# Last feed-forward part of a two-block network: high and low stream in one product of 512 columns

## The chip, the cores and the metric

One core of a Trainium2 chip runs the whole program. The metric is the device time of one execution in microseconds; the times shown are of three runs.

## What is computed

The input is 256 tokens of 1024 features; 16 meta tokens are put ahead of them (272 in all). A first block of two layers (each: feed-forward, mixer, feed-forward) is followed by a second block with attention, a recurrent mixer and 32 routed experts. All is float32. The part that the change touches is the last feed-forward part of the second layer, and the residual around it:

```python
def swiglu(x, w_gate, w_up, w_down):
    return (jax.nn.silu(x @ w_gate) * (x @ w_up)) @ w_down

h = h + 0.5 * swiglu(rmsnorm(h, ffn2_norm[l]), ffn2_w_gate[l], ffn2_w_up[l], ffn2_w_down[l])
```

with 1024 features, 2816 hidden ones, and (here) only the 256 real tokens, since the meta tokens aren't used after it.

## The kernel before, in words

Features lie on the 128 partitions, tokens on the columns. Numbers of full precision are split for the matrix engine into a high part of type fp32r and a low part (the rest), and one product of float32 becomes three of fp32r: `product` (L741 to L745) does w_hi x_hi (L743), w_hi x_lo (L744) and w_lo x_hi (L745), all added up in one PSUM bank. Each needs a weight load of its own.

**A feed-forward part** is `ffn(f, n)` on every engine, f = 0 to 3; the last is f = 3, with `window(3)` = 16, so `t:T` are 256 columns (272 in the others). It has 22 hidden tiles j. For each the weights of gate and of up are one *half* each: a tile of 128 x 1024 in one of 7 ring slots (two halves a slot), split into one of four buffers `w_split`. Half 2j is gate, half 2j + 1 is up; a half is 8 chunks of 3 products (`features`, L773; the first two halves go chunk by chunk, `first_two`, L763). Pair j writes PSUM banks 2(j % 4) and 2(j % 4) + 1. Then come 22 *down* parts of 8 outputs times 3 products, which add into the 8 banks; the last two are done output by output (L821 to L827).

**The order of each queue is written out by hand**, and each engine works its queue in order:

- TensorE waits for the low split of a half, from pair 4 on for the eviction of the pair four before (L794), and ahead of half 4 does the norm's sum (`norm_sum`, L735), for which ScalarE squares and GpSimd adds (L2791). In pair j = 14 (`CTX_AT`) it also sums squares for the second block into bank 5, and half 29, which has that bank, waits until ScalarE has copied the sum out as `ctx_r` (L800).
- ScalarE (L1585 to L1600), per pair: at j = 14 first the copy `ctx_r` (L1590); from j = 2 on the high splits of the halves 2j + 4 and 2j + 5 (`weights_hi`, L1506, each once the half four before is used); the Silu of gate j (L1594) once VectorE has evicted it; for j = 2 to 9 the high copy of hid j - 2 (L1569).
- VectorE (L2087 to L2107), per pair: the low splits of the same two halves (`weights_lo`, L1975); the eviction of gate (L2092) and of up (L2094) from PSUM, each times 1/rms (`rstd`); a drain; once the Silu is there, hid = up x gate (L2102); for j = 2 to 9 the low copy of hid j - 2 (`hidden_lo`, L2084).
- In the down parts both go on with the splits of weights and of the other tiles of hid. At the end `residual` (L1985) adds half of each output bank to h; ScalarE squares h (L1734) for the norm of the second block, which TensorE sums with plain fp32 products (L1060), and GpSimd adds the same squares (L2856).
- GpSimd adds up squares of the context (L2843, L2846) at the start of this part.
- SyncE loads the weights, a slot at a time, once the low splits of the slot's former contents are done.

The plain fp32 products of the second block (L1066 with 512 columns, L1072 with 256, L1367 with 128) stand in the trace as two records each, and each record has a weight load.

The first lines of VectorE's eviction, as they are before:

```python
dve.wait_ge(split_used, n0 + 2 * j + 1)
nc.vector.tensor_tensor(gate_act[:, j % 4, t:T], ps[:, bank, 0:T - t], rstd[:, t:T], ALU.mult).then_inc(gate_ready, 1)
dve.wait_ge(split_used, n0 + 2 * j + 2)
used = nc.vector.tensor_tensor(hid[:, j, t:T], ps[:, bank + 1, 0:T - t], rstd[:, t:T], ALU.mult)
```

Of the kernel before, what the change touches and what calls it, by code (L numbers as in the profile page):

```python
# [14 lines left out]
C = D // P  # L15
META, SEQ = 16, 256
T = META + SEQ
DEPTH = 2
FF = 2816
F = FF // P  # L20
# [9 lines left out]
SPLITS = 4  # L30
# [8 lines left out]
HID_SPLITS = 8  # L39
# [191 lines left out]
def build(nc, stream_ffn, stream_in, stream_out, stream_mod, stream_in2, stream_out2, stream_expert,  # L231
# [4 lines left out]
    with ExitStack() as ctx:  # L236
# [3 lines left out]
        def sem(name):  # L240
            return ctx.enter_context(nc.semaphore(name))
# [47 lines left out]

        rest = 3 * C * T  # L290
        h = cut(arena, 0, C, T)
        x_hi = parts("x_hi", arena_at + 4 * C * T, C, T)
        x_lo = parts("x_lo", arena_at + 4 * 2 * C * T, C, T)
        w_split = [parts(f"w_split{b}", ring_at + 4 * (NS + b) * SLOT, 2, C, P) for b in range(SPLITS)]
        X_AT = (NS + SPLITS) * SLOT
        m = layout(ring, X_AT, [("rv", 3, 512), ("rstd", T)])
# [3 lines left out]
        m = layout(arena, rest, [("hid", F, T), ("gate", 4, T)])  # L300
        hid, gate_act = m["hid"], m["gate"]
        warm = cut(arena, rest, 513)
        hid_hi = parts("hid_hi", arena_at + 4 * (rest + (F + 4) * T), HID_SPLITS, T)
        hid_lo = parts("hid_lo", arena_at + 4 * (rest + (F + 4 + HID_SPLITS) * T), HID_SPLITS, T)
        assert rest + (F + 4 + 2 * HID_SPLITS) * T <= ARENA
        ffn_sq = hid[:, F - C:]

# [35 lines left out]
        stat_ready, dev_ready, factor_ready, normed, last_normed, back_ready, y_hi_ready, y_split_ready = (  # L343
            sem(x) for x in ("stat_ready", "dev_ready", "factor_ready", "normed", "last_normed", "back_ready", "y_hi_ready", "y_split_ready"))
        lam_dots_ready, lam_exp_ready = sem("lam_dots_ready"), sem("lam_exp_ready")


        raw2 = h[:, :, META:T]
# [376 lines left out]
        def _(pe):  # L725
# [15 lines left out]
            def product(to, w, k, hi, lo, first, last_):  # L741

                pe.matmul(to, w[:, 0, k], hi, start=first, stop=False)  # L743
                pe.matmul(to, w[:, 0, k], lo, start=False, stop=False)  # L744
                return pe.matmul(to, w[:, 1, k], hi, start=False, stop=last_)  # L745

            def split_half(n):

                pe.wait_ge(split_ready, n + 2)
                return w_split[n % SPLITS]  # L750
# [12 lines left out]
            def first_two(n, n0, banks, t=0):  # L763

                both = [split_half(n0), split_half(n0 + 1)]
                for c in range(C):
                    pe.wait_ge(x_split_ready, n * C + c + 1)
                    for k in range(2):
                        last = product(ps[:, banks[k], 0:T - t], both[k], c, x_hi[:, c, t:T], x_lo[:, c, t:T], c == 0, c == C - 1)
                        if c == C - 1:  # L770
                            last.then_inc(split_used, 1)

            def features(n, bank, t=0):  # L773

                w = split_half(n)
                for c in range(C):
                    last = product(ps[:, bank, 0:T - t], w, c, x_hi[:, c, t:T], x_lo[:, c, t:T], c == 0, c == C - 1)
                last.then_inc(split_used, 1)

            def ffn(f, n):  # L780

                n0 = HALF_AT["ffn", f, 0]
                t = window(f)
                if f == 0:
                    first_of_all(n0)
                else:
                    first_two(n, n0, (0, 1), t)
                for j in range(1, F):
                    if j == 2 and f > 0:
                        norm_sum(n)  # L790
                    if j == 3:
                        pe.wait_ge(std_ready, n + 1)
                    if j >= 4:
# [12 lines left out]
                down = n0 + 2 * F  # L806

                def part(i, o):
                    return product(ps[:, o, 0:T - t], w_split[(down + i) % SPLITS], o, hid_hi[:, i % HID_SPLITS, t:T],
                                   hid_lo[:, i % HID_SPLITS, t:T], i == 0, i == F - 1)  # L810

                for i in range(F - 2):
                    split_half(down + i)
                    pe.wait_ge(hid_split_ready, f * F + i + 1)
                    for o in (4, 5, 6, 7, 0, 1, 2, 3) if i == 0 else range(C):
                        if i == 0 and o % 2 == 0:
                            pe.wait_ge(gate_up_used, f * F + F - 3 + (o - 4) % C // 2)
# [673 lines left out]
        def _(act):  # L1491
# [42 lines left out]
            def ffn(f, n):  # L1534
# [52 lines left out]
                for j in range(F):  # L1587
                    if f == 2 * DEPTH - 1 and j == CTX_AT:
                        act.wait_ge(ctx_summed, 1)
                        nc.scalar.activation(ctx_r, ps[:, 2 * (j % 4) + 1, 0:SEQ], ACT.Copy).then_inc(ctx_std_ready, 1)  # L1590
                    if j >= 2:
                        weights_hi(n0 + 2 * j + 6)
                    act.wait_ge(gate_ready, f * F + j + 1)
                    nc.scalar.activation(gate_act[:, j % 4, t:T], gate_act[:, j % 4, t:T], ACT.Silu).then_inc(gate_act_ready, 1)  # L1594
                    if 0 <= j - 2 < HID_SPLITS:
                        hidden_hi(j - 2)
                    for half in range(2):
                        if j - half in units:
                            mod_products(units[j - half], half)
# [362 lines left out]
        def _(dve):  # L1962
# [73 lines left out]
            def ffn(f, n):  # L2036
# [50 lines left out]
                for j in range(F):  # L2087
                    if j >= 2:
                        weights_lo(n0 + 2 * j + (6 if j < F - 1 else 5))
                    bank = 2 * (j % 4)  # L2090
                    dve.wait_ge(split_used, n0 + 2 * j + 1)
                    nc.vector.tensor_tensor(gate_act[:, j % 4, t:T], ps[:, bank, 0:T - t], rstd[:, t:T], ALU.mult).then_inc(gate_ready, 1)  # L2092
                    dve.wait_ge(split_used, n0 + 2 * j + 2)
                    used = nc.vector.tensor_tensor(hid[:, j, t:T], ps[:, bank + 1, 0:T - t], rstd[:, t:T], ALU.mult)  # L2094
                    if j in PORTIONS[f]:
                        used = mod_collect(PORTIONS[f][j], bank + 1)
                    used.then_inc(gate_up_used, 1)
                    if j == F - 1:
                        weights_lo(n0 + 2 * j + 6)
                    dve.drain()  # L2100
                    dve.wait_ge(gate_act_ready, f * F + j + 1)
                    nc.vector.tensor_tensor(hid[:, j, t:T], hid[:, j, t:T], gate_act[:, j % 4, t:T], ALU.mult).then_inc(hid_ready, 1)  # L2102
                    if 0 <= j - 2 < HID_SPLITS:
                        hidden_lo(j - 2)
                    if f == 0 and j == 8:
                        lambda_weights()
                    if j - 2 in units:  # L2107
                        mod_add(units[j - 2])
# [10 lines left out]
                for o in range(C):  # L2119
                    if o < C - 1:  # L2120
                        dve.wait_ge(y_ready, f * (C - 1) + o + 1)
                    else:
                        dve.wait_ge(split_used, down + F)
                    residual(o, o, 0.5, t)
                    if o >= 1 and f < 2 * DEPTH - 1:
                        stream_lo(n + 1, o - 1)
# [869 lines left out]
```

## Time and profile before

| what | value |
|---|---|
| time, median of 3 runs | 1739.18 us (1738.33 to 1740.95) |
| span of the profiled execution | 1737.7 us, 30185 instructions |
| what lies around the span, to the median | 1.5 us |
| TensorE busy (weight loads) | 1713.1 us, 99% (1408.5 us, 81%) |
| VectorE, ScalarE, GpSimd busy | 978.2, 797.4, 169.4 us |
| mean granted TensorE clock | 0.998 |
| chain that ended last | TensorE 88%, DMA 6% |

The span runs from the first to the last instruction of one profiled execution, which has no time of its own beside it; the runs are timed apart. Engines: PE is TensorE, PEld its weight loads, DVE VectorE, ACT ScalarE, POOL GpSimd, SP SyncE. A matmul's record is longer than its pitch, since matmuls are pipelined: what counts is the distance from one start to the next. The last feed-forward part goes from about 904 us to 1094 us; its down parts start at 1032.

### The profile page before, as it was taken

Reading aid. Unit: us, or ns where it says so; the run is one execution under the profiler, and the core shown is the slowest. Engines: PE = TensorE matmul, PEld = TensorE weight load, DVE = VectorE, ACT = ScalarE, POOL = GpSimd, SP = SyncE. Lnnn points to the kernel's source line nnn. Section 1 sums busy time; section 2 is a strip of 40 time slices with the busy share of each in tenths; the row PEclk is TensorE's granted clock in tenths of the full one; section 3 lists DMA queues with packets and bytes.
Section 4 is the critical chain, followed back from the end, with each engine's and each line's share of the span. In section 5 each row is a group of like instructions: output and inputs, shape, how many; then the busy total and the mean of one; then the engine's idle time right before and its main releaser. Section 6 shows DMA issues by size and latency. Waiting matters only on the chain.

```text
span 1737.7 us, 30185 instructions
## 1 busy us (share of the span) xinstructions
PE 1713.1 (99%) x12315; PEld 1408.5 (81%) x12316; DVE 978.2 (56%) x1689; ACT 797.4 (46%) x1432; POOL 169.4 (10%) x173
## 2 busy tenths in 40 slices
PE   9999999999999999999999999999999999999998
PEld 8999998999999999998999999677764544444443
DVE  6776577678766777678778666475732111121111
ACT  6664455466656765665455445354621111111111
POOL 1000053210000100014314000100410000000000
PEclk9999999999999999999999999999999999999999
DMA  9555552244566576574336555132299999999997
GB/s 384 198 228 209 170 166 103 98 172 163 224 259 249 191 270 243 196 247 141 117 130 228 190 177 176 49 85 73 114 420 404 428 427 428 428 428 428 428 427 304
DMA packets 78817, 425.87 MB, mean 245 GB/s; under 512 B 16352, under 2 KB 32992, under 8 KB 41824
## 3 DMA queue, kind: packets, MB, share of 16 engines
q1 hardware_dynamic: 78256, 421.01, 62.3%
q10 hardware_dynamic: 432, 3.08, 0.4%
q8 instruction: 89, 1.46, 0.3%
q14 instruction: 40, 0.33, 0.1%
HBM read 423.02 MB, written 1.05 MB: 244 GB/s over the span
## 4 chain that ended last, share of the span: by engine, by line
PE 88%; DMA 6%; DVE 2%; ACT 2%; issue 1%; DVEq 0%; SPq 0%; POOL 0%; POOLq 0%; ACTq 0%
PE ps L743 18%; PE ps L745 18%; PE ps L744 18%; PE ps L1393 10%; PE ps L1444 5%; DMA ring<-stream_expert 5%; PE ps L1367 3%; PE ps L1072 2%; PE ps L1066 2%; PE ps L1078 2%; DVE w_split L1975 1%; ACT w_split L1506 1%; PE ps L1374 1%; PE ps L1375 1%; PE ps L921 0%
## 5 line engine op out<-in xcount | busy, mean ns | idle before, releaser
L1975 DVE TENSOR_TENSOR w_split<-ring,w_split 128x1024 fp32r<-128x1024 f32 x335 | 421.1, 1276 | 250.3 <-ACT w_split L1506 249.7
L743 PE MATMUL ps<-x_hi,w_split 128*128 128x272 f32 (+1 forms) x1856 | 541.7, 292 | 4.7 <-DVE arena L2171 2.1
L745 PE MATMUL ps<-x_hi,w_split 128*128 128x272 f32 (+1 forms) x1856 | 534.0, 288 | 0.0
L744 PE MATMUL ps<-x_lo,w_split 128*128 128x272 f32 (+1 forms) x1856 | 532.1, 287 | 0.0
L1506 ACT ACTIVATE w_split<-ring 128x1024 fp32r<-128x1024 f32 x335 | 345.5, 1052 | 234.7 <-PE ps L745 233.2
L743 PEld LDWEIGHTS ps<-x_hi,w_split 128*128 128x128 f32 x1856 | 350.3, 189 | 12.2 <-issue 4.8
L744 PEld LDWEIGHTS ps<-x_lo,w_split 128*128 128x128 f32 x1856 | 350.2, 189 | 0.3
L745 PEld LDWEIGHTS ps<-x_hi,w_split 128*128 128x128 f32 x1856 | 350.1, 189 | 0.0
L745 PE MATMUL ps<-hid_hi,w_split 128*128 128x272 f32 (+1 forms) x704 | 201.6, 286 | 0.0
L744 PE MATMUL ps<-hid_lo,w_split 128*128 128x272 f32 (+1 forms) x704 | 201.5, 286 | 0.0
L743 PE MATMUL ps<-hid_hi,w_split 128*128 128x272 f32 (+1 forms) x704 | 201.1, 286 | 0.0
L1393 PE MATMUL ps<-ring,arena 128*64 128x512 f32 x704 | 187.4, 594 | 3.5 <-DMA ring<-stream_expert 2.8
L1393 PEld LDWEIGHTS ps<-ring,arena 128*64 128x64 f32 x704 | 58.9, 137 | 98.7 <-issue 93.5
L2724 DVE TENSOR_TENSOR arena<-arena,ps 128x512 f32<-128x512 f32 x16 | 11.0, 687 | 217.4 <-PE ps L1393 217.4
L743 PEld LDWEIGHTS ps<-hid_hi,w_split 128*128 128x128 f32 x704 | 132.7, 189 | 0.0
L744 PEld LDWEIGHTS ps<-hid_lo,w_split 128*128 128x128 f32 x704 | 132.5, 188 | 0.0
L745 PEld LDWEIGHTS ps<-hid_hi,w_split 128*128 128x128 f32 x704 | 132.5, 188 | 0.0
L1594 ACT ACTIVATE arena<-arena 128x272 f32<-128x272 f32 (+1 forms) x88 | 37.6, 427 | 151.8 <-DVE arena L2092 151.3
L1902 ACT ACTIVATE arena<-ps,small 128x128 f32<-128x128 f32 x64 | 24.0, 456 | 163.4 <-PE ps L1367 163.4
L1582 ACT ACTIVATE ring<-ring,small 128x256 f32<-128x256 f32 x192 | 81.3, 494 | 0.0
L1444 PE MATMUL ps<-ring,arena 128*64 128x512 f32 x352 | 78.0, 595 | 0.0
L2735 DVE SCALAR_TENSOR_TENSOR ye_lo<-ps,arena,ye_hi 128x512 fp32r<-128x512 f32 x32 | 24.0, 750 | 91.4 <-ACT ye_hi L1918 76.5
(438 smaller groups left out, 2362.8 us busy)
## 6 DMA issues: line engine op xcount, KB each, us to landing
ring<-stream_ffn SPq DMA_DIRECT2D x131, 1024.0 KB, 4.9
ring<-stream_expert SPq DMA_DIRECT2D x48, 2048.0 KB, 25.1
ring<-stream_expert SPq DMA_DIRECT2D x36, 1024.0 KB, 12.6
arena<-stream_expert SPq DMA_DIRECT2D x16, 2048.0 KB, 25.5
ring<-stream_in SPq DMA_DIRECT2D x27, 1024.0 KB, 4.8
ring<-stream_mod SPq DMA_DIRECT2D x24, 1024.0 KB, 4.9
con<-stream_expert SPq DMA_DIRECT2D x8, 2048.0 KB, 26.2
ring<-stream_out SPq DMA_DIRECT2D x12, 1024.0 KB, 5.0
```

Source lines behind the costliest of these rows:

```text
L743: pe.matmul(to, w[:, 0, k], hi, start=first, stop=False)
L744: pe.matmul(to, w[:, 0, k], lo, start=False, stop=False)
L745: return pe.matmul(to, w[:, 1, k], hi, start=False, stop=last_)
L1066: last = pe.matmul(ps[:, b, 0:KEYS], w[:, c], x2n[:, :, c], start=c == 0, stop=c == C - 1)
L1072: last = pe.matmul(ps[:, b, i * SEQ:i * SEQ + SEQ], w[:, i, c], x2n[:, 0, c], start=c == 0, stop=c == C - 1)
L1367: last = pe.matmul(ps[:, 6 + half, (c % 4) * P:(c % 4) * P + P], h2t[:, t, c * P:c * P + P], sel[:, t], start=t == 0, stop=t == 1)
L1393: last = pe.matmul(ps[rows, 4 + part, 0:FE], xs[:, c, rows], w, start=c == 0, stop=c == C - 1)
L1444: last = pe.matmul(ps[rows, 6 + half, 0:512], hidT[:, f, rows], w[:, half * 512:half * 512 + 512], start=f == 0, stop=f == FE // P - 1)
L1506: nc.scalar.activation(w_split[n % SPLITS][:, 0], half_of(n), ACT.Copy).then_inc(hi_ready, 1)
L1582: last = nc.scalar.activation(to[:, c], w[:, c], ACT.Identity, scale=cc[:, c, v:v + 1])
L1594: nc.scalar.activation(gate_act[:, j % 4, t:T], gate_act[:, j % 4, t:T], ACT.Silu).then_inc(gate_act_ready, 1)
L1975: nc.vector.tensor_tensor(w[:, 1], half_of(n), w[:, 0].bitcast(fp32), ALU.subtract).then_inc(split_ready, 1)
```

## The change

In parts with `t` > 0, which is the last feed-forward part alone, high and low stream lie in one tensor, `x_both` and `hid_both`, and w_hi is multiplied with both in one product of 2 x 256 columns, which fills a PSUM bank: columns 0 to 255 for the high, 256 to 511 for the low stream. w_lo x_hi is added to columns 0 to 255. For gate and up ScalarE copies the low half of a bank to SBUF as soon as its half is done, between its splits; VectorE adds the high half to it, and multiplies by 1/rms in SBUF, in two further operations behind a drain. The low copy of hid moves ahead of the wait for the Silu. At the end VectorE adds the low half of each output bank to h, drains, and adds the high half. The mixers call `product` themselves and stay as they are.

```diff
+            def wide_product(bank, w, k, both, first, last_):
+
+                hi_last = last_ and not first
+                if not hi_last:
+                    pe.matmul(ps[:, bank, 0:2 * SEQ], w[:, 0, k], both, start=first, stop=False)
+                last = pe.matmul(ps[:, bank, 0:SEQ], w[:, 1, k], both[:, 0], start=False, stop=False)
+                if hi_last:
+                    last = pe.matmul(ps[:, bank, 0:2 * SEQ], w[:, 0, k], both, start=False, stop=True)
+                return last
...
 def features(n, bank, t=0):
                 for c in range(C):
-                    last = product(ps[:, bank, 0:T - t], w, c, x_hi[:, c, t:T], x_lo[:, c, t:T], c == 0, c == C - 1)
+                    if t:
+                        last = wide_product(bank, w, c, x_both[:, :, c, t:T], c == 0, c == C - 1)
...
 def part(i, o):
+                    if t:
+                        return wide_product(o, w_split[(down + i) % SPLITS], o, hid_both[:, :, i % HID_SPLITS, t:T], i == 0, i == F - 1)
...
 scalar, for j in range(F):
-                    if j >= 2:
-                        weights_hi(n0 + 2 * j + 6)
+                    for k in range(2):
+                        if t:
+                            act.wait_ge(split_used, n0 + 2 * j + k + 1)
+                            to = gate_act[:, j % 4, t:T] if k == 0 else hid[:, j, t:T]
+                            nc.scalar.activation(to, ps[:, 2 * (j % 4) + k, SEQ:2 * SEQ], ACT.Copy).then_inc(low_copied, 1)
+                        if j >= 2:
+                            weights_hi(n0 + 2 * j + 5 + k)
                     act.wait_ge(gate_ready, f * F + j + 1)
...
 vector, for j in range(F):
+                    if t:
+                        gate_at, up_at = gate_act[:, j % 4, t:T], hid[:, j, t:T]
+                        dve.wait_ge(low_copied, LOW_BEFORE + 2 * j + 1)
+                        nc.vector.tensor_tensor(gate_at, ps[:, bank, 0:SEQ], gate_at, ALU.add)
+                        dve.wait_ge(low_copied, LOW_BEFORE + 2 * j + 2)
+                        used = nc.vector.tensor_tensor(up_at, ps[:, bank + 1, 0:SEQ], up_at, ALU.add)
+                        dve.drain()
+                        nc.vector.tensor_tensor(gate_at, gate_at, rstd[:, t:T], ALU.mult).then_inc(gate_ready, 1)
+                        nc.vector.tensor_tensor(up_at, up_at, rstd[:, t:T], ALU.mult)
+                        if 0 <= j - 2 < HID_SPLITS:
+                            hidden_lo(j - 2)
...
 vector, the outputs
+                    if t:
+                        nc.vector.scalar_tensor_tensor(h[:, o, t:T], ps[:, o, SEQ:2 * SEQ], 0.5, h[:, o, t:T], ALU.mult, ALU.add)
+                        dve.drain()
                     residual(o, o, 0.5, t)
```

`first_two` is changed as `features` is.

## Rows read from the trace of the kernel before

**Rows 1.** Stretches: us; busy time of each engine (instructions); granted clock, DMA share, GB/s.
```profile
933.80:985.60 51.80, 51.80 (x440) 51.80 (x440) 35.82 (x55) 25.02 (x36) 0.00 (x0) 1.00 0.56 197
...
1290.00:1737.70 447.70, 435.58 (x2370) 206.90 (x2366) 73.59 (x159) 70.42 (x158) 1.42 (x2) 1.00 0.98 413
```

**Rows 2.** Timeline of TensorE, gate and up products: start us, us, instruction.
```profile
949.73 0.28 PE L743 MATMUL ps<-x_hi,w_split 128*128 128x256 f32 x1
...
951.15 0.28 PE L743 MATMUL ps<-x_hi,w_split 128*128 128x256 f32 x1
```

**Rows 3.** Chain that ended last, in order of time: start us, us, plain fp32 products.
```profile
1117.31 13.81 PE ps L1066 x32
1131.12 13.81 PE ps L1072 x64
...
1302.83 1.98 PE ps L1367 x16
1305.25 1.79 PE ps L1367 x16
```

**Rows 4.** Timeline of TensorE, the norm's sum ahead of half 4.
```profile
916.93 0.70 PE L739 MATMUL ps<-arena,con 128*128 128x272 f32 x2 [0.72 <-POOL arena L2791]
```

**Rows 5.** Timelines of ScalarE and VectorE, one pair in the steady state.
```profile
951.76 1.06 ACT L1506 ACTIVATE w_split<-ring 128x1024 fp32r<-128x1024 f32 x1 [1.32 <-PE ps L745]
954.45 0.42 ACT L1594 ACTIVATE arena<-arena 128x256 f32<-128x256 f32 x1 [1.62 <-DVE arena L2092]
954.77 0.40 ACT L1569 ACTIVATE hid_hi<-arena 128x256 fp32r<-128x256 f32 x1
955.08 1.04 ACT L1506 ACTIVATE w_split<-ring 128x1024 fp32r<-128x1024 f32 x1
...
952.85 1.22 DVE L1975 TENSOR_TENSOR w_split<-ring,w_split 128x1024 fp32r<-128x1024 f32 x1 [1.15 <-ACT w_split L1506]
954.00 0.42 DVE L2092 TENSOR_TENSOR arena<-ps,ring 128x256 f32<-128x256 f32 x1
954.33 0.41 DVE L2094 TENSOR_TENSOR arena<-ps,ring 128x256 f32<-128x256 f32 x1
954.90 0.42 DVE L2102 TENSOR_TENSOR arena<-arena 128x256 f32<-128x256 f32 x1 [0.15 <-ACT arena L1594]
```

**Rows 6.** Timeline of ScalarE, two high splits in a row.
```profile
923.38 1.99 ACT L1506 ACTIVATE w_split<-ring 128x1024 fp32r<-128x1024 f32 x2
```

**Rows 7.** Timelines of ScalarE and TensorE around half 29.
```profile
988.85 0.36 ACT L1590 ACTIVATE more<-ps 128x256 f32<-128x256 f32 x1
989.11 1.06 ACT L1506 ACTIVATE w_split<-ring 128x1024 fp32r<-128x1024 f32 x1
...
989.27 0.39 PE L743 MATMUL ps<-x_hi,w_split 128*128 128x256 f32 x1 [0.25 <-ACT more L1590]
```

**Rows 8.** Timeline of VectorE at the start of the part.
```profile
919.34 1.84 DVE L1989 RECIPROCAL ring<-ring 128x272 f32<-128x272 f32 x1
921.26 0.42 DVE L2092 TENSOR_TENSOR arena<-ps,ring 128x256 f32<-128x256 f32 x1
...
923.51 0.82 DVE L2102 TENSOR_TENSOR arena<-arena 128x256 f32<-128x256 f32 x1 [0.16 <-ACT arena L1594]
924.46 3.10 DVE L1975 TENSOR_TENSOR w_split<-ring,w_split 128x1024 fp32r<-128x1024 f32 x2
```

**Rows 9.** TensorE's timeline at the program's start, then two stretches behind it.
```profile
9.93 0.40 PE L743 MATMUL ps<-x_hi,w_split 128*128 128x272 f32 x1 [1.87 <-DVE x_lo L1980]
...
10.00:12.00 2.00, 2.00 (x9) 1.85 (x10) 1.74 (x4) 2.00 (x5) 0.00 (x0) 0.55 1.01 417
12.00:14.00 2.00, 2.00 (x11) 1.86 (x11) 1.23 (x1) 1.00 (x2) 0.00 (x0) 0.60 1.00 416
```

**Rows 10.** VectorE's timeline at the end of the part; the chain, norm's product.
```profile
1091.07 0.42 DVE L1985 SCALAR_TENSOR_TENSOR arena<-ps,arena 128x256 f32<-128x256 f32 x1 [0.28 <-PE ps L745]
...
1094.53 3.45 PE ps L1060 x16
```

More of the change, by code:

```diff
@@ L291, in build @@
         h = cut(arena, 0, C, T)
-        x_hi = parts("x_hi", arena_at + 4 * C * T, C, T)
-        x_lo = parts("x_lo", arena_at + 4 * 2 * C * T, C, T)
+        x_both = parts("x_both", arena_at + 4 * C * T, 2, C, T)
+        x_hi, x_lo = x_both[:, 0], x_both[:, 1]
         w_split = [parts(f"w_split{b}", ring_at + 4 * (NS + b) * SLOT, 2, C, P) for b in range(SPLITS)]
@@ L302, in build @@
         warm = cut(arena, rest, 513)
-        hid_hi = parts("hid_hi", arena_at + 4 * (rest + (F + 4) * T), HID_SPLITS, T)
-        hid_lo = parts("hid_lo", arena_at + 4 * (rest + (F + 4 + HID_SPLITS) * T), HID_SPLITS, T)
+        hid_both = parts("hid_both", arena_at + 4 * (rest + (F + 4) * T), 2, HID_SPLITS, T)
+        hid_hi, hid_lo = hid_both[:, 0], hid_both[:, 1]
         assert rest + (F + 4 + 2 * HID_SPLITS) * T <= ARENA
@@ L345, in build @@
         lam_dots_ready, lam_exp_ready = sem("lam_dots_ready"), sem("lam_exp_ready")
+        low_copied, LOW_BEFORE = lam_exp_ready, 1
         raw2 = h[:, :, META:T]
@@ L768, in first_two @@
                     for k in range(2):
-                        last = product(ps[:, banks[k], 0:T - t], both[k], c, x_hi[:, c, t:T], x_lo[:, c, t:T], c == 0, c == C - 1)
+                        if t:
+                            last = wide_product(banks[k], both[k], c, x_both[:, :, c, t:T], c == 0, c == C - 1)
+                        else:
+                            last = product(ps[:, banks[k], 0:T], both[k], c, x_hi[:, c], x_lo[:, c], c == 0, c == C - 1)
                         if c == C - 1:
@@ L776, in features @@
                 for c in range(C):
-                    last = product(ps[:, bank, 0:T - t], w, c, x_hi[:, c, t:T], x_lo[:, c, t:T], c == 0, c == C - 1)
+                    if t:
+                        last = wide_product(bank, w, c, x_both[:, :, c, t:T], c == 0, c == C - 1)
+                    else:
+                        last = product(ps[:, bank, 0:T], w, c, x_hi[:, c], x_lo[:, c], c == 0, c == C - 1)
                 last.then_inc(split_used, 1)
@@ L2091, in ffn @@
                     dve.wait_ge(split_used, n0 + 2 * j + 1)
-                    nc.vector.tensor_tensor(gate_act[:, j % 4, t:T], ps[:, bank, 0:T - t], rstd[:, t:T], ALU.mult).then_inc(gate_ready, 1)
-                    dve.wait_ge(split_used, n0 + 2 * j + 2)
-                    used = nc.vector.tensor_tensor(hid[:, j, t:T], ps[:, bank + 1, 0:T - t], rstd[:, t:T], ALU.mult)
+                    if t:
[9 more added lines that the diff above has]
+                            hidden_lo(j - 2)
+                    else:
+                        nc.vector.tensor_tensor(gate_act[:, j % 4], ps[:, bank, 0:T], rstd, ALU.mult).then_inc(gate_ready, 1)
+                        dve.wait_ge(split_used, n0 + 2 * j + 2)
+                        used = nc.vector.tensor_tensor(hid[:, j], ps[:, bank + 1, 0:T], rstd, ALU.mult)
                     if j in PORTIONS[f]:
@@ L2102, in ffn @@
                     nc.vector.tensor_tensor(hid[:, j, t:T], hid[:, j, t:T], gate_act[:, j % 4, t:T], ALU.mult).then_inc(hid_ready, 1)
-                    if 0 <= j - 2 < HID_SPLITS:
+                    if t == 0 and 0 <= j - 2 < HID_SPLITS:
                         hidden_lo(j - 2)
@@ L2123, in ffn @@
                         dve.wait_ge(split_used, down + F)
+                    if t:
+                        nc.vector.scalar_tensor_tensor(h[:, o, t:T], ps[:, o, SEQ:2 * SEQ], 0.5, h[:, o, t:T], ALU.mult, ALU.add)
+                        dve.drain()
                     residual(o, o, 0.5, t)
```

## The prediction

> **What bounds the kernel now.** I read the stages first, then TensorE's pitch, then who waits for whom in the last feed-forward part. In the table of stretches TensorE is busy for all 51.80 us of the gate and up products [rows 1], and from 1290 us on weight traffic runs at 413 GB/s beside TensorE; those loads are gated by work of the second block, so whatever the last feed-forward part gains or loses shifts all that follows. In the timeline twelve products of 256 columns start in 951.15 - 949.73 = 1.42 us, 118.3 ns each [rows 2]. At a granted clock of 1.00, which is 2.4 GHz [rows 1], 256 columns are 106.7 ns: 11.6 ns of each are not columns. That excess is all the change can take from TensorE, for the columns stay (3 x 256 = 512 + 256).
>
> **What it takes away.** Two products per chunk instead of three. What does one of 512 columns cost when the weights of the next are loaded beside it? No such product is in the trace. The nearest rows: the records of plain fp32 products, two cycles a column, each with a weight load. With 256 columns (213.3 ns of streaming) 13.81 us / 64 = 215.8 ns, excess 2.5; with 512 columns 13.81 / 32 = 431.6 ns; with 128 columns (106.7 ns) 1.98 / 16 = 124 or 1.79 / 16 = 112 ns, excess 5 to 17 [rows 3]. So the excess is large where streaming is about as long as the load beside it and small where it is twice as long. I take 215.8 for the 512-column product and keep 118.3 for the 256-column one: 334.1 against 354.9, **20.8 ns saved per triple**. Ends: 0 (the excess goes by columns, as 431.6 is exactly twice 215.8) and 31.2 (all at the fp32 pace: 215.8 + 107.9). A fixed excess per product would be 11.6.
>
> By the Trainium skill, TensorE: Matmul & The Clock Gate, section "Back-to-back issue gap", a warm product takes N/2.4 + 2.5 ns, so a merge would save 2.5 ns a triple; here 256 columns take 118.3, not 109.2, so the page does not describe these products.
>
> **Where that saving counts.** Not in halves 0 to 3: half 4 waits for the norm's sum, which waits for GpSimd (0.72 us idle [rows 4]), and GpSimd for squares that the change doesn't touch. Those 32 triples only lengthen the wait. A half (8 triples) then takes 2.67 us, a pair 5.35 (before 5.68).
>
> **What it adds to the other engines.** Per pair j: two ScalarE copies from PSUM, each behind a wait for its half and ahead of the weight split; on VectorE two adds in place of two evictions (same shape and place, same price), a drain, and two multiplies within SBUF. Behind ScalarE's wait stand its splits, the Silu, the hi copies and at j = 14 ctx_r; the first two lead to VectorE's next low split.
>
> The loop that decides goes from one Silu to the next, because both queues are in order. Its links before, from start to start [rows 5]: hi split to low split 952.85 - 951.76 = 1.09, low split to gate eviction 954.00 - 952.85 = 1.15, eviction to Silu 954.45 - 954.00 = 0.45, Silu to what follows it 0.32, the hi copy of hid 955.08 - 954.77 = 0.31 (only for j = 2 to 9), and hi split to hi split 1.99 - 1.05 = 0.94 [rows 6]. Sum 3.95, or 4.26 with the hi copy, against a TensorE pair of 5.68: ScalarE has over a microsecond to spare and splits run ahead.
>
> Added to the loop: two PSUM copies at 0.26 (the one such copy, ctx_r: 989.11 - 988.85 [rows 7]); the second add, 0.33 (954.33 - 954.00 [rows 5]); then until the gate multiply the add's 0.41 and a drain of 0.08 (the reciprocal ends at 919.34 + 1.84 = 921.18, the next starts at 921.26 [rows 8]). The multiply takes the eviction's 0.45 to the Silu (0.42 long [rows 5]). Together 0.52 + 0.33 + 0.49 = 1.34. **The loop becomes 5.60 us for j = 2 to 9 and 5.29 after**, against a TensorE pair of 5.35. So the spare time is gone, and a lag once made isn't made up. The low copy of hid, now ahead of VectorE's wait for the Silu, waits for ScalarE's hi copy behind that Silu; VectorE's own round grows to some 5.1 and stays below the loop. SyncE's refills wait for the low splits, but run seven slots (seven pairs, 39 us) ahead of their use, at a DMA share of 0.56 [rows 1]: cost 0.
>
> The lag is made at the start. VectorE begins pair 0 at 921.26 and reaches the splits of j = 2 at 924.46, pausing only 0.16 for each Silu [rows 8]. While GpSimd works (no longer from 933.8 on [rows 1]) a multiply within SBUF takes up to 0.82 [rows 8] instead of 0.42 [rows 5]. Pairs 0 and 1 get two more each, plus the drain: 2 x (0.15 + 2 x 0.75) = 3.3, less 0.1 of idle. Splits of j = 2 then start at 927.7, end at 930.7 (1.5 each there [rows 8]), adds and drain 0.82, multiply 0.85: Silu of j = 2 at 932.4. To the Silu of j = 13 are 8 x 5.60 + 3 x 5.29 = 60.7: **993.1**. Before it is at 988.53, one 0.32 ahead of ctx_r at 988.85 [rows 7]: 4.6 us later.
>
> That Silu matters because ScalarE copies ctx_r out of PSUM right behind it, and TensorE can't start half 29, whose bank it is, before: now 0.25 us of idle, at 989.27 [rows 7]. With the change half 29 starts 4.6 us later. I add 0.5 (between 0 and 1), since GpSimd, met by more work of VectorE, keeps it slow a little longer: **+5.1 us**. The stalls on splits in halves 8 to 28 lie within it.
>
> **Clock.** Before half 29 TensorE now stands still for nearly 5 us. At the start of the program, after 1.87 us of idle, the granted clock is 0.55 and 0.60 in the next two stretches of 2 us [rows 9]: (0.45 + 0.40) x 2 = **1.7 us** lost, at the level of 1.2 GHz. I take that; ends 0 and 2.
>
> **What is left to gain.** From half 29 TensorE sets the pace again: 15 halves and 22 down parts, 37 x 8 = 296 triples x 20.8 ns = **-6.2 us**. The banks for the first down part need pair 21's adds: at most 0.2.
>
> **The tail.** The last residuals become two operations with a drain: 0.41 + 0.08 + 0.33 = 0.82 per output against TensorE's 6 x 118 = 0.71, now 0.67 [rows 10]. Over eight outputs VectorE ends 8 x 0.82 - 7 x 0.67 = 1.9 us behind. The norm's product takes the squares one by one over 3.45 us [rows 10]; its eighth step starts 3.0 us after its first, its square is there after 1.9 + 0.45 = 2.35. Cost 0; with that cover gone 0.5.
>
> **Sum.** +5.1 + 1.7 - 6.2 = +0.6 us. It is made against the profiled span of 1737.7 us; the median, 1739.2, lies 1.5 above it and moves with it: **1739.8 us**.
>
> **Rivals.** A difference of 0.2% (3.5 us) is about what a measurement tells from none.
> - *The excess goes by columns* (or the wide product loads its weights twice, so that the change does not do what it says). Nothing is saved: +6.8, **1746.0**. For it: 431.6 = 2 x 215.8. Against: 118.3 against 215.8 / 2. Chance 0.12. It is slower from a saving under 11 ns a triple on. The page's rule is the nearest to it, 2.5 x 296 = 0.7 us saved.
> - *Fixed excess per product, and a longer loop.* 11.6 ns saved gives -3.4 instead of -6.2, in sum +3.4; and each 0.1 us that a wait or drain puts on the loop is 1.1 us at half 29, the place where it is paid: **1743.7** with 0.1. For it: the loop has no gap left, and any wait between two engines that I left out adds to it; against: the wide product has streaming enough to cover a load. Chance 0.20, four fifths of it beyond 1742.7.
> - *No lag.* If VectorE's start were not late, ScalarE's copies would go into its idle time, half 29 would be late by the added 0.8 only, and 320 + 176 = 496 triples count: -10.3 + 0.8, **1729.7**. Against: VectorE's start has next to no gaps to fill [rows 8], and the loop exceeds the pair. Chance 0.10.
> - *As forecast*, 1735.7 to 1742.7: 0.52. The remaining 0.06 is spread evenly over the three.
>
> **How the numbers follow.** Low end: 31.2 ns saved (gate and up then held by the loop of 5.29: 7 x 0.39 + 22 x 0.25 = 8.4) and no clock loss: 5.1 - 8.4 = -3.3, 1735.9. High end: the first rival, 1746. Range 1735.5 to 1746. Faster by over 0.2%: 0.10 + 0.02 = 0.12; within: 0.52 + 0.04 + 0.02 = 0.58; slower: 0.12 + 0.16 + 0.02 = 0.30.
>
> **What would show it.** A triple at 334 ns in the down part; the pair's pace 5.6 us for j below 10; Silu of j = 13 near 993; half 29 waiting some 5 us for ctx_r with a lower clock behind it; down part starting some 4 us later than 1032 and ending near 1095. Wrong if low splits run ahead of TensorE at j = 10, if the wait at half 29 stays under 2 us, or if a triple takes over 345 ns.

## The result, and where the time went

| | kernel before | changed kernel |
|---|---|---|
| median, 9 runs each | 1739.34 us | 1744.41 us |
| lowest to highest | 1738.33 to 1740.95 | 1742.70 to 1746.79 |
| span of the profiled execution | 1737.7 us | 1744.8 us (its run: 1746.55) |
| granted clock, mean of the span | 0.998 | 0.995 |

The changed kernel is slower: ratio 1.0028, with a 95% interval from 1.002 to 1.0037, or 5.1 us. The forecast was 1739.8 us, within a range that reaches to 1746.0.

The profiled execution of the changed kernel is some 2 us above its median. The norm's sum, which was at 916.93 [rows 4], is now at 919.30, 2.4 us later, and this comes from the start of the program, far ahead of the changed part. In the chains that ended last the same weight split stands at 33.41 us before and at 35.77 us after, and between 12 and 20 us TensorE is granted less clock: 0.50 in each of the two stretches of 2 us, then 0.66, where the trace of before has 0.60 [rows 9] and then 1.00. The traces of experiments 3, 6 and 7 have 1.00 in all these stretches, so this differs from one execution to the next and isn't the change's. The 2.4 us are taken off below wherever a time of after stands against one of before. In order: the split before and after, the stretch after, the norm's sum after.

```profile
33.41 1.05 ACT w_split L1506
...
35.77 1.05 ACT w_split L1525
...
16.00:20.00 4.00, 4.00 (x24) 4.00 (x24) 2.75 (x6) 4.00 (x10) 3.15 (x3) 0.66 1.02 430
...
919.30 0.70 PE L740 MATMUL ps<-arena,con 128*128 128x272 f32 x2 [0.82 <-POOL arena L2830]
```

The stretches of [rows 1], and two more around half 29 (columns as there):

```profile
933.80:985.60 51.80, 51.09 (x291) 44.27 (x290) 43.35 (x74) 28.47 (x54) 0.73 (x1) 1.00 0.53 185
985.60:995.00 9.40, 6.71 (x38) 5.59 (x37) 7.43 (x13) 5.41 (x10) 0.00 (x0) 0.99 0.54 210
995.00:1000.00 5.00, 3.30 (x10) 2.81 (x11) 2.82 (x6) 1.91 (x4) 0.00 (x0) 0.50 0.58 210
```

VectorE's busy time in the first of them has gone from 35.82 to 43.35 us. The stretch has 291 products and 290 weight loads, so a wide product doesn't load its weights twice. In the third TensorE is granted a clock of 0.50, which is its level of 1.2 GHz. The timelines of ScalarE, then of VectorE, for one pair in the steady state, answer to [rows 5]:

```profile
951.77 0.42 ACT L1618 ACTIVATE arena<-arena 128x256 f32<-128x256 f32 x1 [2.48 <-DVE arena L2123]
...
957.41 0.42 ACT L1618 ACTIVATE arena<-arena 128x256 f32<-128x256 f32 x1 [2.48 <-DVE arena L2123]
...
953.75 2.45 DVE L1999 TENSOR_TENSOR w_split<-ring,w_split 128x1024 fp32r<-128x1024 f32 x2 [0.28 <-ACT w_split L1525]
956.11 0.42 DVE L2119 TENSOR_TENSOR arena<-ps,arena 128x256 f32<-128x256 f32 x1
956.44 0.42 DVE L2121 TENSOR_TENSOR arena<-ps,arena 128x256 f32<-128x256 f32 x1
956.95 0.42 DVE L2123 TENSOR_TENSOR arena<-arena,ring 128x256 f32<-128x256 f32 x1
```

From one Silu (L1618) to the next are 957.41 - 951.77 = 5.64 us, and the Silu waits 2.48 us for the gate multiply (L2123). That multiply stands behind two low splits, two adds and a drain. The round is the loop that the prediction wrote out, and neither of its two engines is busy all the time. Then ScalarE and TensorE around half 29, where [rows 7] had 0.25 us of idle:

```profile
995.96 0.42 ACT L1618 ACTIVATE arena<-arena 128x256 f32<-128x256 f32 x1 [2.48 <-DVE arena L2123]
996.28 0.37 ACT L1609 ACTIVATE more<-ps 128x256 f32<-128x256 f32 x1
996.70 0.79 PE L752 MATMUL ps<-x_both,w_split 128*128 128x512 f32 x1 [4.40 <-ACT more L1609]
...
998.15 0.63 PE L752 MATMUL ps<-x_both,w_split 128*128 128x512 f32 x1
...
998.79 0.63 PE L752 MATMUL ps<-x_both,w_split 128*128 128x512 f32 x1
...
1001.88 0.39 PE L752 MATMUL ps<-x_both,w_split 128*128 128x512 f32 x1
```

TensorE stands still for 4.40 us until ctx_r has been copied out (L1609), and then a triple takes 998.79 - 998.15 = 0.64 us for the whole of half 29. The first product of the down parts, and what follows their last:

```profile
1040.94 0.39 PE L752 MATMUL ps<-hid_both,w_split 128*128 128x512 f32 x1
...
1102.79 1.46 PE L1079 MATMUL ps<-arena,ring 128*128 128x256 f32 x6
```

For the gate and up products at full clock a whole pair is read, since one triple is too short for the trace's steps of 0.01 us. The chain that ended last marks the end of each pair's second half:

```profile
1007.15 0.24 PE ps L753 x2
1012.73 0.24 PE ps L753 x2
...
1102.95 3.45 PE ps L1079 x16
```

1012.73 - 1007.15 = 5.58 us for 16 triples, 348.8 ns each: **6.1 ns saved** in the gate and up products. The 176 triples of the down parts take 1102.79 - 1040.94 = 61.85 us, 351.4 ns each. Before they took 1094.37 - 1031.98 = 62.39 us, so **3.1 ns** are saved there.

The account up to the norm's product, in the two profiled executions: half 29 starts 996.70 - 989.27 - 2.4 = 5.0 us later; it takes 1001.88 - 996.70 = 5.18 us instead of 2.85, 2.3 more; the 14 halves behind it give back 0.8 and the down parts 0.5. Sum +6.0; the chain has 1102.95 - 1094.53 - 2.4 = 6.0. From there to the end the kernels of this study take between 641.6 and 643.5 us, without an order that I could find. The medians are only 5.1 us apart. Part of the difference to 6.0 is the clock of half 29, which is not the same in every execution: in the trace of experiment 7 TensorE waits as long ahead of it, 4.38 us, but the half takes 998.52 - 994.07 = 4.45 us, 1.6 more than before and not 2.3:

```profile
994.07 0.50 PE L753 MATMUL ps<-x_both,w_split 128*128 128x512 f32 x1 [4.38 <-ACT more L1611]
...
998.52 0.39 PE L753 MATMUL ps<-x_both,w_split 128*128 128x512 f32 x1
```

What is left of it is within the scatter of the rest of the program.

### The profile page after: what moved, and what is told of

The parts are those of the page before. It is cut to its first block, busy times and chain, and to the rows that moved or that the text cites. A ratio compares the mean times of both kernels' runs of the same rounds, so it can differ in the third digit from the quotient of the medians.

```text
span 1744.8 us, 29277 instructions
## 1 busy us (share of the span) xinstructions
PE 1715.0 (98%) x11787; PEld 1385.6 (79%) x11788; DVE 999.9 (57%) x1741; ACT 808.6 (46%) x1476; POOL 167.7 (10%) x173
## 4 chain that ended last, share of the span: by engine, by line
PE 82%; DMA 6%; DVE 5%; ACT 3%; DVEq 2%; issue 1%; SPq 0%; POOL 0%; ACTq 0%; POOLq 0%
PE ps L744 14%; PE ps L746 14%; PE ps L745 14%; PE ps L1412 10%; PE ps L1463 5%; DMA ring<-stream_expert 5%; PE ps L752 4%; PE ps L1386 3%; DVE w_split L1999 2%; PE ps L753 2%; PE ps L1091 2%; PE ps L1085 2%; ACT w_split L1525 2%; PE ps L1097 2%; DVEq L2122 1%
## 5 line engine op out<-in xcount | busy, mean ns | idle before, releaser
L744 PE MATMUL ps<-x_both,w_split 128*128 128x272 f32 (+1 forms) x1504 | 443.1, 295 | 5.6 <-DVE arena L2210 2.1
L746 PE MATMUL ps<-x_both,w_split 128*128 128x272 f32 (+1 forms) x1504 | 435.5, 290 | 0.0
L745 PE MATMUL ps<-x_both,w_split 128*128 128x272 f32 (+1 forms) x1504 | 433.4, 288 | 0.0
L744 PEld LDWEIGHTS ps<-x_both,w_split 128*128 128x128 f32 x1504 | 284.3, 189 | 12.8 <-issue 4.8
L745 PEld LDWEIGHTS ps<-x_both,w_split 128*128 128x128 f32 x1504 | 284.6, 189 | 0.2
L746 PEld LDWEIGHTS ps<-x_both,w_split 128*128 128x128 f32 x1504 | 284.0, 189 | 0.0
L1412 PE MATMUL ps<-ring,arena 128*64 128x512 f32 x704 | 187.4, 594 | 3.4 <-DMA ring<-stream_expert 2.7
L746 PE MATMUL ps<-hid_both,w_split 128*128 128x272 f32 x528 | 152.2, 288 | 0.0
L745 PE MATMUL ps<-hid_both,w_split 128*128 128x272 f32 x528 | 152.2, 288 | 0.0
L744 PE MATMUL ps<-hid_both,w_split 128*128 128x272 f32 x528 | 151.7, 287 | 0.0
L752 PE MATMUL ps<-x_both,w_split 128*128 128x512 f32 x308 | 112.6, 402 | 5.8 <-ACT more L1609 4.4
L1618 ACT ACTIVATE arena<-arena 128x272 f32<-128x272 f32 (+1 forms) x88 | 37.6, 428 | 169.8 <-DVE arena L2128 116.0
L744 PEld LDWEIGHTS ps<-hid_both,w_split 128*128 128x128 f32 x528 | 99.4, 188 | 0.0
L745 PEld LDWEIGHTS ps<-hid_both,w_split 128*128 128x128 f32 x528 | 99.3, 188 | 0.0
L746 PEld LDWEIGHTS ps<-hid_both,w_split 128*128 128x128 f32 x528 | 99.3, 188 | 0.0
L753 PE MATMUL ps<-x_both,w_split 128*128 128x256 f32 x352 | 92.8, 284 | 0.0
```

Source lines behind the costliest of these rows:

```text
L752: pe.matmul(ps[:, bank, 0:2 * SEQ], w[:, 0, k], both, start=first, stop=False)
L753: last = pe.matmul(ps[:, bank, 0:SEQ], w[:, 1, k], both[:, 0], start=False, stop=False)
L1412: last = pe.matmul(ps[rows, 4 + part, 0:FE], xs[:, c, rows], w, start=c == 0, stop=c == C - 1)
```

## The experiments

**Theory S**: the saving is small by itself, because a product of 512 columns costs about 231 ns, nearly two of 256. **Theory L, with K**: ScalarE's lag costs TensorE its 4.4 us at one place only, the copy of ctx_r, and the clock behind it costs 2.3 us more. **Theory O**: the lag comes from the order of VectorE's work in the loop. Each had a rival. A line of after is named as it stands there; edits shift the numbers by a few.

**1. The wide products without the work they bring.**

```diff
-   nc.scalar.activation(to, ps[:, 2 * (j % 4) + k, SEQ:2 * SEQ], ACT.Copy)
...
-   nc.vector.tensor_tensor(gate_at, ps[:, bank, 0:SEQ], gate_at, ALU.add)
...
-   nc.vector.tensor_tensor(gate_at, gate_at, rstd[:, t:T], ALU.mult)
+   nc.vector.tensor_tensor(gate_act[:, j % 4, t:T], ps[:, bank, 0:T - t], rstd[:, t:T], ALU.mult)
...
-   nc.vector.scalar_tensor_tensor(h[:, o, t:T], ps[:, o, SEQ:2 * SEQ], 0.5, h[:, o, t:T], ALU.mult, ALU.add)
```

> Edit: the products of 512 columns stay, but the low halves (PSUM columns 256 to 511) are never added: ScalarE's low copies, VectorE's two adds, the drain, the multiplies in place and the extra residual step are gone, and VectorE evicts columns 0 to 255 times rstd as before the change. The output lacks the high weights times the low stream. Theory S (a triple of products saves only 5 to 6 ns, because a 512-column product costs about 231 ns by itself): the time is 496 x 5.2 ns = 2.6 us under the kernel before, 1736.5 to 1737.5, ratio to it about 0.9985; triples stand at 0.35 us in the trace and half 29 starts without the 4.4 us wait. Rival P (the 512-column product would take 213 ns, and what slows it is the extra work of ScalarE and VectorE beside it): triples at 0.334 us and 10 us under the kernel before, near 1729.

Measured: 1736.95 us against 1739.51 of before on the same chip, ratio 0.9983 (0.9974 to 0.9991). The group of TensorE's wide gate and up products from 903 to 1100 us (busy us, mean ns of one | idle before them and what ended it):

```profile
L752 PE MATMUL ps<-x_both,w_split 128*128 128x512 f32 x308 | 110.1, 395 | 0.4 <-ACT more L1609 0.3
```

Nearly nothing is waited for, and in the chain the pairs still end 5.58 us apart, with ScalarE and VectorE free of all the added work:

```profile
1002.54 0.24 PE ps L753 x2
1008.12 0.24 PE ps L753 x2
```

The wide product is not slowed by the work beside it; rival P falls. What TensorE alone can win is 2 to 3 us.

**2. All that work, with narrow products.**

```diff
-   pe.matmul(ps[:, bank, 0:2 * SEQ], w[:, 0, k], both, start=first, stop=False)
+   pe.matmul(ps[:, bank, 0:SEQ], w[:, 0, k], both[:, 0], start=first, stop=False)
+   pe.matmul(ps[:, bank, SEQ:2 * SEQ], w[:, 0, k], both[:, 1], start=False, stop=False)
```

> Edit: all of the change's work on ScalarE and VectorE stays, but the triple is three products of 256 columns again, the low one into PSUM columns 256 to 511. Theory S: half 29 is set by ScalarE, not by the products, so only the 296 triples behind it cost, 5.2 ns each: 1.5 us over the changed kernel, near 1746, and the wait before half 29 shrinks from 4.4 to about 3.2 us. Theory P or any theory in which the wide product saves 15 to 20 ns a triple that something else ate: 4.5 to 6 us over the changed kernel, near 1750.

Measured: 1746.61 us, ratio to before 1.004 (1.0027 to 1.0053): 7.1 us over before, about 2 over the changed kernel. TensorE's timeline at half 29, and the stretch around it:

```profile
996.21 0.58 PE L750 MATMUL ps<-x_both,w_split 128*128 128x256 f32 x1 [3.95 <-ACT more L1605]
...
995.00:1000.00 5.00, 3.79 (x17) 3.80 (x18) 2.41 (x4) 1.91 (x4) 0.00 (x0) 0.50 0.61 210
```

The start of half 29 and the fall of the clock are the same without a single wide product: ScalarE sets them. The wait is 3.95 us, 0.45 less than in the changed kernel, and not 1.2 less as expected. The expectation counted all 200 triples from half 4 to half 28. But in both kernels TensorE waits for a low split at 938 us, and the end of that stall is VectorE's, so only the 152 triples behind it count, 0.9 us. And in the changed kernel the pairs that follow take longer than 5.58 us. These are the last products of two of its halves, twelve halves apart:

```profile
946.49 0.39 PE L755 MATMUL ps<-x_both,w_split 128*128 128x512 f32 x1
...
980.30 0.39 PE L755 MATMUL ps<-x_both,w_split 128*128 128x512 f32 x1
```

Six pairs in 980.30 - 946.49 = 33.81 us are 5.64 us each, the round of the loop. It looks as if the low splits hold TensorE there, by less than the list of waits shows; in experiments 5 and 6, where the lag is gone, the pairs take 5.58 us. Against narrow pairs of 5.68 us seven such pairs save 0.04 us each, and the last five halves 0.05 each: 0.5 us in all, about what is measured.

**3. The copy of ctx_r one pair earlier.**

```diff
-   if f == 2 * DEPTH - 1 and j == CTX_AT:
+   if f == 2 * DEPTH - 1 and j == CTX_AT - 1:
+       pe.wait_ge(gate_up_used, f * F + CTX_AT - 3)
        pe.wait_ge(ctx_sq_ready, 1)
-       pe.matmul(ps[:, 2 * (j % 4) + 1, 0:SEQ], ones, ctx_acc, start=True, stop=True)
+       pe.matmul(ps[:, 2 * (CTX_AT % 4) + 1, 0:SEQ], ones, ctx_acc, start=True, stop=True)
```

and ScalarE's copy likewise.

> Edit: TensorE issues the ones product of the context's squares at the start of pair 13 instead of 14 (still into bank 5), and ScalarE copies it out before pair 13's work; half 29 keeps its wait for that copy. Theory L (ScalarE's lag reaches TensorE only through this copy, and costs the idle time and the clock after it): the 4.4 us wait before half 29 is gone, the granted clock stays at 0.98 or more there, and the time is 5 to 6.7 us under the changed kernel, 1738 to 1739.5, no more than 1 us off the kernel before. Rival B (the lag reaches TensorE elsewhere as soon as this copy is out of the way, at the bank waits or at the start of the down parts): the idle time shows up at those waits, and less than 2 us is won.

Measured: 1738.57 us, ratio to before 0.9997 (0.9988 to 1.0006). TensorE's waits from 903 to 1100 us (us in total, times, longest), and the stretches from 985.6 us on:

```profile
PE ps L752 <- DVE w_split L2000: 1.2, 2, 0.7
PE ps L752 <- DVE arena L2122: 0.9, 1, 0.9
PE ps L740 <- POOL arena L2831: 0.8, 1, 0.8
...
985.60:995.00 9.40, 9.40 (x57) 8.27 (x56) 7.45 (x14) 4.45 (x10) 0.00 (x0) 1.00 0.48 158
995.00:1000.00 5.00, 5.00 (x31) 4.37 (x30) 4.29 (x7) 2.53 (x6) 0.00 (x0) 1.00 0.57 179
1000.00:1036.00 36.00, 35.10 (x201) 30.61 (x200) 28.97 (x48) 19.74 (x35) 0.00 (x0) 1.00 0.57 198
```

The wait for ctx_r and the low clock are gone, and nearly 6 us with them, though the lag itself is untouched: the Silu still waits 2.47 us. One new wait appears, at the adds that free a bank (L2122, the second of them): 0.9 us, in the last stretch, whose clock stays at 1.00. Theory L holds for most of the loss, and its rival for the rest, which is more than that 0.9: against experiment 6, where the lag is gone too, the norm's product starts 2.1 us later behind the norm's sum (1094.66 - 916.74 against 1092.49 - 916.71). Besides the 0.9 these are the longer waits for low splits (1.2 against 0.7 us) and the pairs of 5.64 us.

**4. TensorE kept busy through the gap.**

```diff
    if f == 2 * DEPTH - 1 and j == CTX_AT and k == 1:
+       pe.wait_ge(gate_up_used, f * F + j - 2)
+       for _ in range(9):
+           pe.matmul(ps[:, 7, SEQ:2 * SEQ], ones, ctx_acc, start=True, stop=True)
        pe.wait_ge(ctx_std_ready, 1)
```

The first added line waits until bank 7, which the filler writes, is free.

> Edit: in the gap before half 29 TensorE runs nine fp32 products of 256 columns (ones by the context's squares, into a bank half that nobody reads, about 9 x 0.43 = 3.9 us), then waits as before. Theory K (the low clock after the idle time costs its own 2.3 us): half 29 starts at the same time after ScalarE's copy, but its triples take 0.35 us and not 0.64, and the time is about 2.3 us under the changed kernel, near 1742. Rival N (the clock falls for another reason than the idle engine, or what it loses is hidden behind later waits): the time stays within 0.5 us of the changed kernel.

Measured: 1742.28 us, 2.1 under the changed kernel; ratio to before 1.0015 (1.0006 to 1.0024). TensorE's timeline:

```profile
990.41 4.05 PE L821 MATMUL ps<-ring,con 128*128 128x256 f32 x18
994.95 0.50 PE L752 MATMUL ps<-x_both,w_split 128*128 128x512 f32 x1 [0.49 <-ACT more L1612]
...
995.40 0.39 PE L752 MATMUL ps<-x_both,w_split 128*128 128x512 f32 x1
...
995.75 0.39 PE L752 MATMUL ps<-x_both,w_split 128*128 128x512 f32 x1
```

Half 29 is as late as ever, but its triples take 995.75 - 995.40 = 0.35 us and not 0.64. The clock's share of the loss is its own, and the idle engine is its cause.

**5. VectorE's second low split behind the gate multiply.**

```diff
+   late = t and 2 <= j < F - 1
    if j >= 2:
-       weights_lo(n0 + 2 * j + (6 if j < F - 1 else 5))
+       weights_lo(n0 + 2 * j + (6 if j < F - 1 and not late else 5))
...
    nc.vector.tensor_tensor(gate_at, gate_at, rstd[:, t:T], ALU.mult).then_inc(gate_ready, 1)
+   if late:
+       weights_lo(n0 + 2 * j + 6)
    nc.vector.tensor_tensor(up_at, up_at, rstd[:, t:T], ALU.mult)
```

> Edit: in the loop VectorE takes the second of the two low weight splits of a pair only behind the gate multiply, where ScalarE's Silu can run beside it; everything else, the copy of the context's sum and its place too, is the changed kernel's. Theory O (the lag is set by the order of VectorE's work ahead of the gate multiply, 5.64 us a round): the round shrinks to some 4.1 to 4.5 us as long as it lags, ScalarE catches up with TensorE, the wait before half 29 falls from 4.4 us to under 1 us and the clock stays up, and the time is 5 to 6.7 us under the changed kernel, 1738 to 1739.5. Rival W (the round is bound by the sum of VectorE's work or by ScalarE, whatever the order): Silus stay 5.3 to 5.6 us apart and less than 1.5 us is won.

Measured: 1736.83 us against 1740.0 of before on that chip, ratio 0.9981 (0.9972 to 0.999), better than forecast. Timelines of ScalarE, then of VectorE for one round:

```profile
940.57 0.42 ACT L1618 ACTIVATE arena<-arena 128x256 f32<-128x256 f32 x1 [1.47 <-DVE arena L2124]
...
945.22 0.42 ACT L1618 ACTIVATE arena<-arena 128x256 f32<-128x256 f32 x1 [1.48 <-DVE arena L2124]
...
952.27 0.38 ACT L1614 ACTIVATE arena<-ps 128x256 f32<-128x256 f32 x1 [0.47 <-PE ps L755]
...
957.85 0.39 ACT L1614 ACTIVATE arena<-ps 128x256 f32<-128x256 f32 x1 [1.40 <-PE ps L755]
...
942.78 1.22 DVE L1999 TENSOR_TENSOR w_split<-ring,w_split 128x1024 fp32r<-128x1024 f32 x1
943.91 0.42 DVE L2120 TENSOR_TENSOR arena<-ps,arena 128x256 f32<-128x256 f32 x1
...
944.75 0.43 DVE L2124 TENSOR_TENSOR arena<-arena,ring 128x256 f32<-128x256 f32 x1
945.10 1.22 DVE L1999 TENSOR_TENSOR w_split<-ring,w_split 128x1024 fp32r<-128x1024 f32 x1
946.23 0.42 DVE L2127 TENSOR_TENSOR arena<-arena,ring 128x256 f32<-128x256 f32 x1
...
947.42 1.22 DVE L1999 TENSOR_TENSOR w_split<-ring,w_split 128x1024 fp32r<-128x1024 f32 x1
```

While it lags, a round takes 945.22 - 940.57 = 4.65 us, a little over the 4.1 to 4.5 expected: in this order VectorE works without a pause (the second split starts 0.35 us behind the gate multiply, the next round's first at 947.42, 4.64 us after this one's), so 4.65 is the sum of its own work. From 952 us on the low copy waits for TensorE (L755): ScalarE has caught up, some 40 us ahead of half 29. The wait there is gone and the clock stays at 1.00.

**6. Both edits together.**

> Edit: both edits together, the ones product and its copy one pair early and the second low split behind the gate multiply. By theories L and O nothing of the lag is left: no wait of TensorE over 0.3 us between the first pair and the end of the down parts, the clock at 1.00 throughout, and 7 to 7.7 us less than the changed kernel, near 1737.3, 1.5 to 2.6 us under the kernel before (ratio about 0.9987), which is the most the wide product has to give by theory S (2.6 us). Rival: the two edits remove the same loss and nothing else stands in the way, so the time is that of either alone, 1738.5 or more, no different from the kernel before.

Measured: 1736.47 us against 1740.0, ratio 0.998 (0.9971 to 0.9989). TensorE's waits from 903 to 1100 us are only these:

```profile
PE ps L740 <- POOL arena L2834: 0.8, 1, 0.8
PE ps L752 <- DVE w_split L2000: 0.7, 2, 0.5
```

The wait for splits, up to 0.5 us, is one more than expected. Against edit 5 alone 0.4 us is within the noise: both edits take the wait at half 29 away, and edit 5 leaves nothing measurable for the other. The reverse doesn't hold: the early copy alone was 0.9 us under its kernel before, the late split alone 3.2 under its own. That half of the rival was right; its time was not.

**7. 512 columns side by side.** The gate and up products stream other values than the reference's.

```diff
-   last = wide_product(bank, w, c, x_both[:, :, c, t:T], c == 0, c == C - 1)
+   at = c * T + t
+   last = wide_product(bank, w, c, x_flat[:, at:at + 2 * SEQ], c == 0, c == C - 1)
```

> Edit: the gate and up products from half 2 on stream 512 columns that lie side by side (256 of one chunk's high stream and the 256 that follow in memory) in place of two pieces 8 chunks apart; the values of these products are not the reference's, the sizes and the number of instructions are the changed kernel's. Theory C (the product is paid by the column, however they lie): pairs stay at 5.58 us, and the time is the changed kernel's within 0.7 us. Rival J (the jump between the two pieces costs 10 to 18 ns each): pairs of 5.3 to 5.4 us from half 29 on, and 1.4 to 2 us less in total.

Measured: 1744.68 us, ratio to before 1.003 (1.0019 to 1.0042), the changed kernel's own. In the chain the pairs end 1009.37 - 1003.79 = 5.58 us apart:

```profile
1003.79 0.24 PE ps L754 x2
1009.37 0.24 PE ps L754 x2
```

The jump between the two pieces costs nothing.

**8 to 10. What the wide product is worth when nothing else is late.** Narrow products with both edits (experiment 2's diff on top of 3 and 5), the kernel before with both edits, and the combined version again, on one chip.

> Edit: the changed kernel with both edits that took the lag away (the ones product and its copy one pair early, the second low split behind the gate multiply), but each triple is three products of 256 columns again, the low one into PSUM columns 256 to 511. TensorE now bounds the whole part, so the difference to the same kernel with the wide product is what the wide product is worth. Theory S: 528 triples x 5.2 ns = 2.7 us over that kernel (1736.5), 1738.5 to 1740, the kernel before within 1 us; pairs 5.68 us apart and not 5.58. Rival P (a wide product is worth 20 ns a triple where nothing else is late): 10 us over it, near 1747.

> Edit: the same two edits in the kernel before, which has neither the wide product nor the work that came with it. Theory S: TensorE waited for only 0.4 us in that kernel's last part, so there is nothing for them to win, and the time is the kernel before's within 0.7 us (ratio 0.9996 to 1.0004). Rival R (what the combined version won over the kernel before comes from the new order and not from the wide product): 2 to 3.5 us under it.

> The combined version once more, beside the two kernels above on the same chip: the wide product with both edits. If its lead is real, it is 1736 to 1737.5, 2 to 3.5 us under the kernel before and 2 to 3.2 us under its twin with three narrow products.

| kernel | us | ratio to before (1739.58) |
|---|---|---|
| narrow, both edits | 1739.75 | 1.0001 (0.9992 to 1.001) |
| before, both edits | 1739.30 | 0.9996 (0.9987 to 1.0005) |
| wide, both edits | 1736.76 | 0.9983 (0.9974 to 0.9992) |

The wide product is worth 3.0 us here; the edits by themselves are worth nothing. By the trace it is somewhat less: from half 4 on 320 triples x 6.1 + 176 x 3.1 = 2.5 us, and the norm's product of the narrow twin starts 2.3 us later than that of experiment 6:

```profile
1094.77 3.45 PE ps L1076 x16
```

```profile
1092.49 3.45 PE ps L1080 x16
```

So there is a version of the change that beats both kernels: wide products, with the second low split behind the gate multiply, and at wish the early copy. With both edits it was measured twice, 3.5 and 2.8 us under the kernel before and 7 to 8 under the changed one.

## Why the prediction was right, and where it was wrong

The time is within the forecast's range, but what put it there is the range's upper end, the rival in which nothing is saved (1746.0, chance 0.12). The forecast itself, 1739.8, was 4.6 us off, by one term of the sum.

- **What bounds the part: right.** TensorE, with 11.6 ns per product to win at most.
- **"What it takes away": wrong, and this step carries the error.** It took 215.8 ns for the 512-column product, from the plain fp32 products, and 20.8 ns saved per triple. The runs show 348.8 and 351.4 ns per triple. With the narrow one left at 118.3 the wide one takes some 230 to 233 ns, 17 to 20 ns over its 213.3 ns of columns: the excess nearly doubles with the columns. The 296 triples behind half 29 gave 120 x 6.1 + 176 x 3.1 = 1.3 us instead of 6.2. Those 4.9 us account for the distance from the forecast of 1739.8 to 1744.4, which is 4.6. Experiments 1 and 7 shut out that the work beside it or the jump in its columns slowed it. The row that spoke for the truth was in the prediction (431.6 = 2 x 215.8); it set its chance at 0.12 because the excess at 256 columns was so much larger than fp32's. But that compared products of two kinds. Of these the trace had only 256 columns and, in the parts ahead, 272, too near to tell: the pairs between 110 and 200 us mostly take 5.97 to 6.06 us, 124.4 to 126.2 ns a product, where a fixed excess of 11.6 would give 124.9 and one by columns 125.7.
- By the Trainium skill, TensorE: Matmul & The Clock Gate, section "Back-to-back issue gap", a merge saves 2.5 ns. Neither of its times for one product fits the rows (109.2 and 215.8 by its rule; 118.3 and some 231 in the traces), but as a saving per triple 2.5 is nearer to the 3.1 and 6.1 measured than my 20.8. The section means this rule for a product by itself; for a stream with weight loads it has about 131 ns at 512 columns, which no row here bears out.
- **The loop: right.** Forecast 5.60 and 5.29 us, measured 5.64 for j up to 10 and 995.96 - 990.63 = 5.33 after. Silu of j = 13 was forecast at 993.1, and with the 2.4 us of the late start 995.5; it is at 995.96. VectorE's own round was put at some 5.1 us; experiment 5 shows it to be 4.65, which left more to win by its order than the prediction saw.
- **Half 29: right.** +5.1 forecast, +5.0 measured. That it is ScalarE's lag, reaching TensorE through this copy, is shown by experiments 2 and 3.
- **The clock: right.** 1.7 us were forecast from a stretch at the program's start. The profiled execution lost 2.3, with half 29 at 0.50 and not at 0.55 to 0.60; that of experiment 7 lost 1.6, and experiment 4 gave 2.1 us back. The rows that the forecast rests on vary as well: the same stretches were at 0.97 and 0.50 in the profile of after.
- **The tail: right.** The two residual operations take 0.83 us per output, and the norm's product isn't held up: 16 steps in 3.45 us, as before.
- **The signs.** By its own signs the prediction is wrong in one point: "if a triple takes over 345 ns". The triples took 348.8 and 351.4, and the 334 that it named never appeared. The down parts start at 1040.94 and end at 1102.79, less 2.4 at 1038.5 and 1100.4, not some 1036 and 1095. The lag of the splits and the wait at half 29 came as described.
- **A slip.** In the low end of the range 7 x 0.39 + 22 x 0.25 is 8.2, not 8.4; no conclusion hangs on it.
- **The rivals.** The time lies between the second (1743.7) and the first (1746.0). The mechanism is close to the first's, the excess goes nearly by columns, while the weights are not loaded twice; the loop was 0.04 us longer than forecast, not 0.1, and a fixed excess, which would save 11.6 ns a triple, isn't what the 6.1 and 3.1 show. Slower by over 0.2% was given 0.30 and came out; no difference was given 0.58, on the strength of the 20.8 ns.

What stays open is what the excess over the columns consists of, 11.6 ns at 256 and 17 to 20 at 512 columns, and why a down triple takes 2.6 ns more than a gate or up triple. No run here tells.

## What to carry to other kernels

Price a merged instruction by the nearest row of its own kind, and where there is none, work the sum out with the end that saves least as well: here the merge was worth 3 us, and the bookkeeping that it needs on two other engines cost over 7 until it was placed well. When work is added to engines with spare time, write out the loop from one instruction to its successor, not their busy shares: VectorE was busy 84% of the time and ScalarE 55%, and the lag was still made. Such a lag costs only where the bound engine needs the late engine, so there are two cures, moving the one late hand-over earlier or taking independent work out from ahead of the instruction that the other engine waits for. Try both; here either removed the long wait and the low clock, but only the second removed the lag itself and made the kernel faster than the one before.

## What the runs showed of the hardware

- A product of 512 fp32r columns takes some 231 ns with a weight load beside it, almost twice the 118.3 ns of one with 256, whether its columns lie in one piece or two.
- After 4.40 and after 3.95 us of idle TensorE was granted 0.50 for the next half; after 4.38 us in experiment 7 the next half was shorter, 4.45 us against 5.18, so the same wait cost 1.6 us in one execution and 2.3 in another. But 0.9 us of idle in experiment 3, and 0.49 us behind filler products in experiment 4, left it at full clock. The filler, plain fp32 products into an unused half bank, held the clock as well as real work does.
- On VectorE, adding a second pass over each 128x256 tile costs 0.33 to 0.35 us of its queue, with a drain between add and multiply 0.51 (956.95 - 956.44); the order in which the same instructions stood made 5.64 or 4.65 us of a round.
